# Closing norm of layer 0 moved into the memory phase of layer 1; attention phase written out, its closing norm tile by tile

## What is computed

```python
for i in range(2):
    h = rmsnorm(x, pre_g[i]); mem_n = rmsnorm(mem, mem_g[i])
    # layer 0: bidirectional SSD over 32 heads; layer 1: neighbourhood attention over 32 heads;
    # both: 4 heads of cross-attention into 256 memory tokens, a SiLU gate, one output projection
    mixed = ssd_branch(h, mem_n, ...) if i == 0 else na_branch(h, mem_n, ...)
    x = x + rmsnorm(mixed @ w_out[i], post_g[i])
```

## Time and profile before

| | us |
|---|---|
| median of 3 runs (2447.37 to 2452.96) | 2452.47 |
| the profiled execution, whole | 2452.85 |
| its span, first to last instruction | 2451.1 |
| PE matmul busy | 2179.7 (89%) |
| DVE busy | 1077.0 (44%) |
| ACT busy | 731.7 (30%) |
| POOL busy | 886.4 (36%) |
| mean granted clock of PE | 0.953 |

### The profile page before, as it was taken

The page is one execution under the profiler, slowest core; times in us unless marked ns, Lnnn a source line. Parts: engine busy times, 40 slices in busy tenths (PEclk is TensorE's granted clock), DMA queues, the critical chain, the costliest instruction groups (busy, mean ns, idle before and its releaser), DMA issues. The chain is left out here.

```text
span 2451.1 us, 33670 instructions
## 1 busy us (share of the span) xinstructions
PE 2179.7 (89%) x13362; PEld 1871.9 (76%) x13362; DVE 1077.0 (44%) x1688; ACT 731.7 (30%) x1659; POOL 886.4 (36%) x618
## 2 busy tenths in 40 slices
PE   6999993889899998985499999699999999999983
PEld 5788872778788787874377887588888888888873
DVE  3112222596777687774531223313443334433334
ACT  4121120443343343332231321033323233332332
POOL 4533330333332242320254333354544445444440
PEclk9999996899999999987699999899999999999997
DMA  5221111243313221322432111122221212212112
GB/s 171 78 61 52 52 35 66 72 120 84 104 60 104 78 95 52 104 69 112 146 85 69 44 52 52 44 66 60 60 66 59 59 59 59 66 59 59 59 34 112
DMA packets 228514, 179.97 MB, mean 73 GB/s; under 512 B 23259, under 2 KB 204795, under 8 KB 228411
## 3 DMA queue, kind: packets, MB, share of 16 engines
q1 hardware_dynamic: 228411, 178.52, 23.4%
HBM read 168.71 MB, written 12.21 MB: 74 GB/s over the span
## 5 line engine op out<-in xcount | busy, mean ns | idle before, releaser
L214 PE MATMUL bank<-Hh,Wh 128*128 128x256 f32 (+1 forms) x2192 | 755.8, 345 | 55.7 <-POOL Wl L191 41.1
L214 PE MATMUL bank<-Hl,Wh 128*128 128x256 f32 (+1 forms) x2192 | 743.1, 339 | 0.0
L188 POOL TENSOR_SCALAR Wh<-Wraw 128x1024 fp32r<-128x1024 f32 x217 | 238.4, 1099 | 1392.7 <-issue 539.5
L214 PE MATMUL bank<-Hh,Wl 128*128 128x256 f32 (+1 forms) x2192 | 741.4, 338 | 0.0
L191 POOL TENSOR_TENSOR Wl<-Wraw,Wh 128x1024 fp32r<-128x1024 f32 x217 | 531.8, 2451 | 18.1
L214 PEld LDWEIGHTS bank<-Hh,Wh 128*128 128x128 f32 x2192 | 421.4, 192 | 103.1 <-POOL Wl L191 41.6
L214 PEld LDWEIGHTS bank<-Hh,Wl 128*128 128x128 f32 x2192 | 420.2, 192 | 44.3
L214 PEld LDWEIGHTS bank<-Hl,Wh 128*128 128x128 f32 x2192 | 421.3, 192 | 40.9 <-issue 1.4
L283 DVE TENSOR_TENSOR acc<-bank,acc 128x512 f32<-128x512 f32 x288 | 198.9, 691 | 274.8 <-PE bank L262 274.0
L262 PE MATMUL bank<-Wh,Mh 128*128 128x512 f32 x576 | 229.9, 399 | 23.8 <-DVE Ml L650 8.5
L262 PE MATMUL bank<-Wh,Ml 128*128 128x512 f32 x576 | 227.1, 394 | 0.0
(11 more groups left out here) (192 smaller groups left out, 2571.1 us busy)
## 6 DMA issues: line engine op xcount, KB each, us to landing
Wraw<-in_na_w_in_dram SPq DMA_DIRECT2D x80, 512.0 KB, 3.6
Wraw<-in_ssd_w_in_dram SPq DMA_DIRECT2D x57, 512.0 KB, 3.8
Wraw<-in_w_out_dram SPq DMA_DIRECT2D x48, 512.0 KB, 3.7
R<-acs_dram SPq DMA_DIRECT2D x16, 1536.0 KB, 6.2
Wraw<-in_w_mem_kv_dram SPq DMA_DIRECT2D x32, 512.0 KB, 3.8
R<-gs_dram SPq DMA_DIRECT2D x32, 128.0 KB, 3.0
macc_dram<-acc SPq DMA_DIRECT2D x1, 3072.0 KB, 9.1
R<-macc_dram SPq DMA_DIRECT2D x1, 3072.0 KB, 12.0
```

What stands on the lines that cost most here:

```text
L188: pool.tensor_scalar(Wh[:, s, :], Wraw[:, s, :], 1.0, 1.0, ALU.mult, ALU.mult).then_inc(pool_c, 1)
L214: mm = pe.matmul(DB[h.k % 2][:, 0:t1 - t0], w[:, k, :], x[:, k, t0:t1], start=(k == 0 and i == 0), stop=(k == KC - 1 and i == 2))
```

## The change

Layer 0's closing norm is no phase of its own any more. Its sums, squares, scalings and residual additions stand in the memory phase of layer 1, beside the K units; `macc` and the residual come tile by tile through two slots each, between the loads of the weight units; `TURN_X = 10` moves the transposes of the x norm from K units to V units; the new layer input is stored to `x1_dram` behind the sixteenth unit's load, and the clearing of `acc` waits for it. In the attention phase the loop is written out for all engines. The output product of pairs 12 and 13 moves from step 14 to behind the scores of step 15. The last pair's output product goes tile by tile over both halves; behind each tile ACT squares it and takes its root, DVE scales it, POOL adds the residual, loaded in step 1, and SP stores it.

```diff
-            vF = [mem[:, 2, 0:512], mem[:, 3, 0:512]]
+            post_gain = r(D)
+            vF = [post_gain[:, 0:512], post_gain[:, 512:1024]]
+            macc, res = mem[:, 0:2, :], mem[:, 2:4, :]
...
-            TURN_X = 2
+            TURN_X = 2 if L == 0 else 10
...
+                        sp.dma_start(post_gain, post_g[0:1, :].broadcast_to([P, D])).then_inc(post_gain_landed, 16)
+
+                    def load_macc(i):
+                        if i >= 2:
+                            sp.wait_ge(summed, i - 1)
+                        sp.dma_start(macc[:, i % 2, :], macc_dram[i * P:(i + 1) * P, :]).then_inc(macc_landed[i % 2], 16)
+
+                    def load_res(i):
+                        if i >= 2:
+                            sp.wait_ge(added, i - 1)
+                        src = x_prompt[0, i * P:(i + 1) * P, :] if i < 2 else x_sample[0, (i - 2) * P:(i - 1) * P, :]
+                        sp.dma_start(res[:, i % 2, :], src).then_inc(res_landed[i % 2], 16)
+
                     for u in range(16):
                         if u == 2:
                             sp.wait_ge(mem_norm.normed, 4)
                             sp.dma_start(gain, pre_g[L:L + 1, :].broadcast_to([P, D])).then_inc(gain_landed, 16)
+                            if L == 1:
+                                for i in range(2):
+                                    load_macc(i)
+                                for i in range(2):
+                                    load_res(i)
+                        if L == 1 and 3 <= u <= 4:
+                            load_macc(2 * u - 4)
+                            load_macc(2 * u - 3)
+                        if L == 1 and 7 <= u <= 10:
+                            load_res(u - 5)
                         load_f(sp, wkv, slice(u * P, (u + 1) * P))
+                    if L == 1:
+                        for i in range(NT):
+                            sp.wait_ge(added, i + 1)
+                        sp.dma_start(x1_dram.rearrange("(i p) c -> p i c", p=P), acc[:, :, :]).then_inc(x1_stored, 16)
...
+                    else:
+                        sp.wait_ge(x1_stored, 16)
...
+                    else:
+                        ss, sd, _ = post
+                        for i in range(NT):
+                            act.wait_ge(summed, i + 1)
+                            if i:
+                                act.wait_ge(post_sums, i)
+                            act.activation(xn[1], acc[:, i, :], ACT.Square, accum_out=ss[:, i:i + 1]).then_inc(post_sums, 1)
+                            if i % 2:
+                                take_k(i // 2)
+                        act.wait_ge(post_sums, NT)
+                        act.activation(sd, ss, ACT.Sqrt, scale=1.0 / D, bias=eps[:, 0:1]).then_inc(post_root, 1)
+                        take_k(3)
+                        x_norm.act_sums(act, xn[1], lambda i: act.wait_ge(added, i + 1),
+                                        lambda i: take_k(4 + i // 2) if i % 2 else None)
+                        take_k(7)
+                        take_v(0)
+                        for u in range(1, 8):
+                            take_v(u)
+                            if u >= 2:
+                                x_norm.act_turned(act, u - 2)
...
+                    else:
+                        for i in range(NT):
+                            dve.wait_ge(macc_landed[i % 2], 16 * (i // 2 + 1))
+                            dve.scalar_tensor_tensor(acc[:, i, :], acc[:, i, :], rssd[:, i:i + 1], macc[:, i % 2, :],
+                                                     ALU.mult, ALU.add).then_inc(summed, 1)
+                        dve.wait_ge(post_gain_landed, 16)
+                        dve.wait_ge(post_root, 1)
+                        c.link(dve.reciprocal(post[2], post[1]))
+                        for i in range(NT):
+                            dve.scalar_tensor_tensor(acc[:, i, :], acc[:, i, :], post[2][:, i:i + 1], post_gain,
+                                                     ALU.mult, ALU.mult).then_inc(post_scaled, 1)
+                            dve.wait_ge(res_landed[i % 2], 16 * (i // 2 + 1))
+                            dve.wait_ge(post_scaled, i + 1)
+                            dve.tensor_tensor(acc[:, i, :], acc[:, i, :], res[:, i % 2, :], ALU.add).then_inc(added, 1)
+                        x_norm.dve_roots(dve, c)
+                        dve.wait_ge(gain_landed, 32)
+                        for u in range(8):
+                            if u < NT:
+                                x_norm.dve_normed(dve, u)
+                            take_v(u)
+                            if u >= 2:
+                                x_norm.dve_low(dve, u - 2)
+                        dve.wait_ge(x1_stored, 16)
...
+                        if u >= TURN_X - 8 >= 0:
+                            x_norm.pe(pe, u - TURN_X + 8)
...
+            OF_END = OF["pe"].k + 7 * 2 * NT + 2
+            LAST = PAIRS - 1
...
-            def steps(eng, counts, step, end):
-                step(0, 0, False)
-                step(1, 1, True)
-                with loop(eng, PAIRS // 2 - 1, counts) as i:
-                    for a in range(2):
-                        step(i * 2 + (2 + a), a, True)
+            def out_after(n):
+                return n % 2 == 0 and 2 <= n < LAST - 1 or n == LAST
+
...
+                for n in range(PAIRS):
+                    step(n, n % 2, n > 0)
...
-                            load_f(sp, w_in, bass.ds(n * P + base, P))
-                        load_f(sp, w_in, bass.ds(n * P + N_K, P))
-                        load_f(sp, w_in, bass.ds(n * P, P))
-                        if a == 0 and prev:
-                            load_out(sp, 1, bass.ds(n * P - 256, 256))
-
-                    steps(sp, [(U["sp"], 10)], step, lambda: load_out(sp, 1, slice(14 * P, 16 * P)))
+                            load_f(sp, w_in, slice(n * P + base, n * P + base + P))
+                        load_f(sp, w_in, slice(n * P + N_K, n * P + N_K + P))
+                        load_f(sp, w_in, slice(n * P, n * P + P))
+                        if n == 1:
+                            sp.dma_start(gain, post_g[1:2, :].broadcast_to([P, D])).then_inc(res_landed, 16)
+                            sp.dma_start(res, x1_dram.rearrange("(i p) c -> p i c", p=P)).then_inc(res_landed, 16)
+                        if out_after(n):
+                            k = (n - 2) // 2 * 256
+                            load_out(sp, 1, slice(k, k + 256))
+
+                    def end():
+                        load_out(sp, 1, slice(14 * P, 16 * P))
+                        for i in range(NT):
+                            sp.wait_ge(done, i + 1)
+                            dst = y_prompt[0, i * P:(i + 1) * P, :] if i < 2 else y_sample[0, (i - 2) * P:(i - 1) * P, :]
+                            sp.dma_start(dst, acc[:, i, :]).then_inc(stored, 16)
+                        sp.wait_ge(stored, 16 * NT)
+
...
-                        for _ in range(4 if a == 0 and prev else 2):
+                        for _ in range(4 if out_after(n) else 2):
...
+                        pool.wait_ge(res_landed, 32)
+                        for i in range(NT):
+                            pool.wait_ge(normed, i + 1)
+                            pool.tensor_tensor(acc[:, i, :], acc[:, i, :], res[:, i, :], ALU.add).then_inc(done, 1)
+
...
+                        if prev and n < LAST:
                             high(n - 1, 1 - a)
+                        elif n == LAST:
+                            act.wait_ge(gated, n)
...
+                        probs(LAST, 1)
+                        act.wait_ge(unit_done, U["act"].value + 2)
+                        high(LAST - 1, 0)
+                        take_pt(LAST)
+                        high(LAST, 1)
+                        out_units()
+                        for i in range(NT):
+                            act.wait_ge(out_added, OF_END + 2 * (i + 1))
+                            if i:
+                                act.wait_ge(squared, i)
+                            act.activation(junk, acc[:, i, :], ACT.Square, accum_out=ss[:, i:i + 1]).then_inc(squared, 1)
+                            act.wait_ge(squared, i + 1)
+                            act.activation(sd[:, i:i + 1], ss[:, i:i + 1], ACT.Sqrt, scale=1.0 / D, bias=eps[:, 0:1])\
+                                .then_inc(rooted, 1)
...
-                            finish(n - 1, 1 - a)
+                            gate(n - 1)
+                            if n < LAST:
+                                low(n - 1, 1 - a)
                         for _ in range(4):
                             U["dve"].next()
                         for _ in range(8):
                             HF["dve"].next()
...
+                        if out_after(n) and n < LAST:
                             dve_out(dve)
                         scores(n)
+                        if n == LAST:
...
-                        finish(15, 1)
```

(58 more changed lines are left out.)

93 lines of the change are left out of this document (51 added, 42 removed).

## The result

2408.65 us, the median of 4 runs (2407.52 to 2412.78), against 2452.72 us (2447.37 to 2455.02) for the kernel before on the same chip: ratio 0.9826, 95% interval 0.9806 to 0.9847. The forecast was 2406.5. The profiled execution has a span of 2407.9 us against 2451.1, 43.2 us less.

The account below looks back on a forecast made before the run. TensorE was taken to bound the attention, so gains lie where it idles. 2452.85 - 32.6 (Part 1) + 3.0 (Parts 2 and 3) - 16.6 (Part 4) = 2406.7; less 0.4 for the median, rounded, 2406.5 us; range 2396 to 2418.

Parts of the forecast that it names:

- Part 1: Layer 0's closing norm inside layer 1's memory phase: loads 39.6 us earlier, less leaks of 7.0, gains 32.6 us (27 to 37).
- the gain's load: Memory phase start: 0.5 MB more ahead of the weights delays GpSimd's first splits, costing 0.9 us (bounds -1 and +2).
- Weight unit 2: Memory phase queue: gain, macc and residual tiles go ahead of this weight load, costing 0.5 us (0 to 3).
- third leak: Memory phase: last residual tile waits for the queue; its square precedes K unit 6's eviction on ScalarE: 1 us (0 to 3).
- The prediction's own sign: Memory phase of layer 1: TensorE would show no gap over 2 us in the K units.
- The last leak: After the last V unit: TensorE waits 3.4 us for the last tile's low half, plus about 1.2 us of lower clock.
- Parts 2 and 3: Attention: loop written out, nothing gained; output product of pairs 12 and 13 moved behind step 15, loss of 3.0 us.
- Part 4: Last output product by tile with the norm: 3.55 us a tile, tail 33.0 us instead of 49.6, gain 16.6 us.
- A: Tail and step 15: VectorE and GpSimd don't exclude each other; 4.0 and 4.3 us more, about 2398; chance 0.18.
- B: K stage: queue is the new bound, weights late and splits held up; leaks grow by 10, about 2416; chance 0.20.
- C: Written-out attention steps: instruction supply costs 3.3 us of TensorE each, slower than before, about 2456; chance 0.02.
- D: Attention loop: hidden branch stalls go, at most some 0.4 us a trip, 3 us in all, 2403.5; chance 0.04.

## Why the prediction came out as it did

- **Part 1, 32.6 us forecast, 27.4 measured.** The queue moved 39.6 us ahead as reckoned. From its first load to T0 it is 25.20 us instead of 24.87: the gain's load cost 0.3, forecast 0.9. Weight unit 2 was not late (forecast 0.5): PE has no gap within the eight K units. The failed step is the third leak. "+1 us (0 to 3)" for the last residual tile and K unit 6 measured 6.4 by its own rows (4.26 + 8.00 - 5.85) and 6.85 by the kernel without it. The queue was blamed for the tile's time; with the rows sooner it stayed. The splits' contention, thought to lie in the bounds, is what the rows show in its place: a scaling and an addition cost 5.3 us a tile at the end, on a VectorE with next to no idle time. The prediction's own sign, no gap over 2 us in the K units, failed with it by the gap of 4.26 behind the last. The last leak is right: a gap of 2.74 where 3.4 stood, 1.47 for the clock where 1.2 did (the four units behind it took 35.07 us, in the kernel before 33.60). Right too is that the transposes cost the same in both places: a K unit with them takes 6.47 us from start to start and one without 5.60, a V unit 7.88 and 7.01, 0.87 each time.
- **Part 1, the sum.** A leak that has no place in the list: K unit 0 took 8.27 us against 7.54, since the granted clock was still at 1.2 GHz for the first 5.7 us from T0, and in the kernel before for 4.0. From T0 to the query units it is 118.43 us against 107.82, 10.6 more: 6.7 by the late eviction (111.71 without it), 3.0 by the last V unit with its wait (10.86 against 7.88), 0.7 by K unit 0, and 0.2 in small pieces. With 0.2 gained between the query units and the attention, 39.6 - 0.3 - 10.6 - 1.5 + 0.2 = 27.4, at the edge of the bounds (27).
- **Parts 2 and 3, zero and a loss of 3.0.** The steps written out lose 0.09 us a pair, in the wait before a step's scores (0.88 against 0.79), 0.6 in all. It is in every kernel that has the steps written out and in neither that has the loop. The increment ahead of Exp is not what makes it (0.88 with it as well); what does was not found. The chain behind step 15 was walked to 42.4 and measured 40.5. Its places are right: PE gaps of 4.15 and 4.28 us, and GpSimd's split beside the normalising. The wrong terms: the first half's last addition ended 15.0 us behind the scores, not 15.6, and GpSimd held VectorE up for 2.35 us (3.85 against 1.50 for six operations), not for the whole 3.4 of a split, so the second half's first addition ended at 21.2 instead of 23.2. From there it went as walked (19.3 us measured, 19.2 forecast). The loss against before was 1.9, and against the same written-out steps with the product left in step 14 it is 3.4, because there the chain is 1.5 us shorter: the table load has left it, which is worth 0.75, and the other half is open. The prediction took the 8.32 us of the earlier trace rows for the alternative and didn't see that the steps' rewriting alone shortens it.
- **Part 4, 16.6 us forecast, 18.4 measured.** The pace was forecast at 3.55 us a tile and is 3.55; the difference is the first tile, whose second half was added 3.7 us after the first matmul and not 5.3, so that its scaling ended at 8.1 and not at 9.8. The prediction put the low clock's cost into tile 0, as in the kernel before (4.44 us for 12 matmuls); here it didn't fall there (2.86). That is luck and no merit of the change: where the clock was low again, in the kernel with the increment, the stage took 32.9 us, against 33.0 forecast. ScalarE's square and table load follow at once, as reckoned:

```profile
2380.46 1.06 ACT L1605 ACTIVATE R<-acc 128x1024 f32<-128x1024 f32 x1 [4.83 <-DVE acc L1699]
...
2381.63 1.28 ACT L1607 ACT_TABLE_LOAD   x1
```

- **The rivals.** A (no exclusion) is refuted in the place where it would have paid: additions 3.55 apart, 2.72 and 2.82 when the scaling is moved or has one input in SBUF. Its price in part 4 was also summed wrongly: at 3.05 us a tile for 3.55 the end comes 5 x 0.5 = 2.5 us sooner and not 4.0. B has its direction right, in that splits and VectorE's operations hold each other up, but it costs through one place in ScalarE's order, and not by late weights. C would have taken 3.3 us a step; 0.045 is there. D is refuted as far as a gain goes: the loop's pair is the shorter one. The Trainium skill's Runtime: NRT & Kernel Launch (Instruction fetch mechanics) says that a taken branch to a page not held stalls instruction fetch; no run here shows such a stall.
- Part 1 fell short by 5.2 us and part 2 by 0.6; parts 3 and 4 were better by 1.1 and 1.8. The span is 3.0 us above the forecast's (2451.1 - 46.2 = 2404.9), less than its largest error: misses of 5.8 us one way and 2.9 the other. That the whole came out so near is in part luck. A slip that bears on nothing: the untouched slice at 3 is the seventh, not the eighth.

## What to carry to other kernels

When work is moved beside a busy stage, add up the engine that takes it at its contended durations, not at the alone ones, and then look at what else stands behind its last piece in each engine's order: here one eviction behind one square cost 6.85 us, and putting the eviction first gave it back. An idle stretch of the main engine that is filled by moving work is a gain only if the chain beneath it gets no longer; here an output product was put into the 8.32 us of waiting, and the chain with it grew by 1.9 us. Where two engines exclude each other, an input put elsewhere can be worth more than another division of labour: 3.4 us with the gain in PSUM against 1.8 with two additions moved.

## What the runs showed of the hardware

- An operation of VectorE with two inputs of 128x1024 in SBUF and one of GpSimd take turns: 3.43 instead of 1.28 and 3.25 instead of 2.34 when both are in steady supply. With the second input in PSUM there was no turn-taking: 1.41 us for two halves throughout. One input in SBUF is not enough by itself: the six normalising operations of step 15, each with one tile as input, took 3.85 us beside GpSimd's split and 1.50 without. The Trainium skill's SBUF — State Buffer (Who interferes with whom) says that an instruction of VectorE with at most one SBUF input doesn't contend with GpSimd outside the 2-port modes. The run with the gain in PSUM agrees, 27.8 us against 31.2; whether the normalising was in such a mode, no run here shows.
- ScalarE's table load of 1.28 us was done ahead of the wait of the operation that needs it when that operation followed the wait directly, and behind it when a semaphore increment stood between.
- A short gap of PE can cost more than itself through the granted clock: 2.74 us of idle were followed by 1.47 us of longer units, 4.26 by 2.15. It is not in proportion and not certain: 4.12 were followed by 1.5 in the kernel with the residual sooner, and of two gaps of 3.43 and 3.44 ahead of the last product one was followed by 1.6 and the other by nothing. In the window of the 4.26 us gap (1216 to 1229) the granted clock's mean is 0.74, idle time included, against 0.94 in the stage before.

```profile
1168.00:1216.00 48.00, 47.68 (x192) 37.62 (x192) 36.48 (x18) 15.80 (x29) 31.27 (x15) 0.94 0.66 217
1216.00:1229.00 13.00, 8.37 (x27) 6.43 (x28) 3.50 (x4) 2.90 (x6) 5.13 (x3) 0.74 0.28 82
```
